# A third late expert: expert 29's results reach token tiles 1 and 0 through TensorE instead of through DRAM

## The chip, the cores and the metric

One core of one Trainium2 chip runs the whole program. The metric is the device time of one execution in microseconds. Engines are named as in the profile: PE is TensorE, DVE is VectorE, ACT is ScalarE, POOL is GpSimd, SP is SyncE, which here only issues DMAs.

## The reference, cut to what matters

Two trunk layers over 256 latent and 256 context tokens, model width 1024. Each layer has a mixer and then a mixture of experts. Layer 0 sends 512 tokens (four tiles of 128) through the experts, layer 1 only the 256 latent ones (tiles 0 and 1). Between them lies layer 1's norm and its input projection; after layer 1 there is only a final norm.

```python
def hierarchical_moe(t, wg, bg, we, be, w1, w3, w2):
    g_logit = (t @ wg + bg); g_sel = argmax(g_logit); g_w = softmax(g_logit)[g_sel]
    e_logit = (t @ we + be).reshape(n, 4, 8)[g_sel]          # 8 experts of the chosen group
    top_p, top_i = lax.top_k(softmax(e_logit), 2)
    top_w = top_p / sum(top_p) * g_w
    for e in range(32):                                       # every token uses two of the 32
        y += combine[:, e] * ((silu(t @ w1[e]) * (t @ w3[e])) @ w2[e])
```

w1, w3 (1024 x 256) and w2 (256 x 1024) are float32, 1 MB each, so one expert is 3 MB of weights.

## The kernel before, in words

The engines run separate programs, written out by hand and tied by semaphores.

**Weights.** SP loads every expert's three matrices as two DMAs of 512 KB each into a ring of 12 slots (`in_ring`, L699). It waits for a free slot (`ring_free`), which PE signals with the first matmul after the last use of a slot. The order is w1, w3 of expert e, then w2 of expert e-1. A few matrices go to spare places loaded ahead.

**One expert.** POOL gathers the rows of up to 64 tokens from DRAM (`gather`, L2523). On PE, `step` (L1154) does for expert e: `T` of the next expert (four transposes, L1067), `Hd` of the previous one (two transposes, L1105), `U` (w1 and w3, 32 matmuls, L1095), `more` (blocks beyond 64 tokens, here three times in all), and `Dn` of the previous expert (w2, 8 matmuls, L1121). ACT and DVE empty PSUM between these. The result goes from PSUM to one of two buffers `YS` by ACT in layer 0 (`copy_y`, L1687) and by DVE in layer 1 (`gated_y`, L2161). POOL scatters it (`scatter`, L2535) to the DRAM tensor `pair_out`, which has for each token one row half per choice.

**The end of the experts.** The results of experts 30 and 31 (`LATE`) do not go to DRAM first. For tiles 1 and 0, DVE builds for each late expert a matrix of one weight per token and slot (`late_slots`, L2163), PE transposes the four of them in one go after `step` of expert 28 (L1176), ACT copies them back (L1691), and in `late_results` (L1180) PE multiplies them with `YS` (L1189) and adds the first choices read back from DRAM (L1194). DVE adds the second choices in `late_pair` (L2202; L2221, L2225, L2226 in layer 0, L2210 and L2217 in layer 1). POOL tells SP (`most_stored`, L2625) when the scatters of experts 0 to 29 have landed, and SP then issues the fetch of the pairs of tiles 1 and 0 (`pairs_back`, L785, four DMAs of 512 KB). In layer 0 POOL scatters experts 30 and 31 after that fetch has landed, for the two context tiles, which SP fetches later (`pairs_stored`).

**The rows of late experts in DRAM.** At the start of the experts of each layer, POOL writes zeros over the rows of the late experts (`late_zeros`, L2539): a memset and one indirect DMA for each late expert (L2544). In layer 0 this stands between the first gathers and the fetch of rows for an extra block of expert 1 (`fetch`, L2559 and L2563), which PE transposes at L1138.

**After layer 0.** PE waits until DVE has updated the first half of tile 0 (L1480), runs fillers (L896), then transposes the normed tiles (L1416).

Of the kernel before, what the change touches and what calls it, by code (L numbers as in the profile page):

```python
# [19 lines left out]
ALU = mybir.AluOpType  # L20
# [263 lines left out]
LATE = (EXPERTS - 2, EXPERTS - 1)  # L284
LATE_TILES = (1, 0)

# [26 lines left out]
def trunk(nc, A):  # L313
# [4 lines left out]
    with ctx:  # L318
# [87 lines left out]
        late_hot = BIASF[:, 512:1024].rearrange("p (t e n) -> p t e n", t=2, e=2)  # L406
        late_T = BIASF[:, 1024:1536].rearrange("p (t e n) -> p t e n", t=2, e=2)
        first_weight = BIASF[:, 1536:1792].rearrange("p (t n) -> p t n", t=2)
# [11 lines left out]
        late_by_choice = small[:, 64:80].rearrange("p (v k t e) -> p v k t e", v=2, k=2, t=2)  # L420
        late_of = small[:, 80:88].rearrange("p (v t e) -> p v t e", v=2, t=2)
# [95 lines left out]
        late_zeroed = sem("late_zeroed")  # L517
        late_hot_ready, late_full, late_ready = sem("late_hot_ready"), sem("late_full"), sem("late_ready")
# [327 lines left out]
        def _(pe):  # L846
# [206 lines left out]
            def experts(l):  # L1053
# [112 lines left out]

                def late_slots():


                    bank = ps[:, 7, :]  # L1170
                    pe.wait_ge(x_y_ready, pe.snap(extras))
                    pe.wait_ge(late_hot_ready, l + 1)
                    for t in (0, 1):
                        for e in (0, 1):
                            at_bank = P * (2 * t + e)
                            mm = pe.transpose(bank[:, at_bank:at_bank + P], late_hot[:, t, e, :], ident)  # L1176
                            freed(mm)
                    mm.then_inc(late_full, 1)

                def late_results():  # L1180

                    banks = {(t, h): open_bank("late", l, t, h) for t, h in LATE_BANKS}
                    pe.wait_ge(late_ready, l + 1)
                    for t in LATE_TILES:
                        for e, expert in enumerate(LATE):
                            pe.wait_ge(y_ready, n0 + expert + 1)
                            for h in (0, 1):
                                p = slice(CAP * h, CAP * (h + 1))
                                mm = pe.matmul(banks[t, h], late_T[p, t, e, :], YS[p, expert % 2, :],  # L1189
                                               start=(e == 0), stop=False)  # L1190
                                freed(mm)
                        for h in (0, 1):
                            pe.wait_ge(y_back[t][h], 16 * (l + 1))
                            close(pe.matmul(banks[t, h], first_weight[:, t, :], back[t][:, D * h:D * h + 512],  # L1194
                                            start=False, stop=True))
# [26 lines left out]
                late_slots()  # L1222
# [3 lines left out]
                Dn(LAST_GROUP, PER_LOOP - 1)  # L1226
                used(LAST_GROUP, PER_LOOP - 1, (2,))
# [317 lines left out]
        def _(act):  # L1545
# [120 lines left out]
            def experts(l):  # L1666
# [13 lines left out]
                def copy_y(i, q):  # L1680
                    n, b = i * PER_LOOP + (n0 + q), q % 2
                    act.wait_ge(y_full, n + 1)

                    act.wait_ge(scattered[b], (i * 2 + (n0 + q) // 2) * 16)
                    if isinstance(i, int) and PER_LOOP * i + q == 1:
                        act.wait_ge(late_zeroed, 32)
                    act.activation(YS[:, b, :], ps[:, 5 + b, :], ACT.Copy).then_inc(y_ready, 1)  # L1687

                def late_slots():
                    act.wait_ge(late_full, l + 1)  # L1690
                    act.activation(late_T.rearrange("p t e n -> p (t e n)"), ps[:, 7, :], ACT.Copy).then_inc(late_ready, 1)  # L1691
# [37 lines left out]
                late_slots()  # L1729
                for q in range(1, PER_LOOP):  # L1730
                    one(LAST_GROUP, q, c[q], ahead=(q + 1 < PER_LOOP))
                if l == 0:
                    copy_y(LAST_GROUP, PER_LOOP - 1)
# [184 lines left out]
        def _(dve):  # L1918
# [126 lines left out]
            def route(l):  # L2045
# [69 lines left out]
                of_late, of_token = choices[:, :, 0:2, LATE[0]:EXPERTS], [P, 2, 2, 2]  # L2115
# [9 lines left out]
            def experts(l):  # L2125
# [29 lines left out]
                def gated_y(i, q):  # L2155
                    n, b = i * PER_LOOP + (n0 + q), q % 2
                    dve.wait_ge(y_full, n + 1)
                    dve.wait_ge(scattered[b], (i * 2 + (n0 + q) // 2) * 16)
                    if isinstance(i, int) and PER_LOOP * i + q == 1:
                        dve.wait_ge(late_zeroed, 64)  # L2160
                    dve.tensor_tensor(YS[:, b, :], ps[:, 5 + b, :], GY, ALU.mult).then_inc(y_ready, 1)  # L2161

                def late_slots():  # L2163


                    dve.wait_ge(routed, l + 1)
                    for t in (0, 1):
                        for e in (0, 1):
                            dve.tensor_scalar(late_hot[:, t, e, :].rearrange("p (h n) -> p h n", h=2),
                                              iota[:, ::-1].unsqueeze(1).broadcast_to([P, 2, CAP]),  # L2170
                                              late_of[:, 1, t, e:e + 1], late_of[:, 0, t, e:e + 1], ALU.is_equal, ALU.mult)
                        ins = dve.tensor_scalar(first_weight[:, t, :], ident, topw[:, t, 0:1], None, ALU.mult)
                    ins.then_inc(late_hot_ready, 1)
# [21 lines left out]
                late_slots()  # L2195
                for q in range(PER_LOOP):
                    one(LAST_GROUP, q, c[q])
                copy_hT(LAST_GROUP, PER_LOOP - 1)
                if l == 1:
                    gated_y(LAST_GROUP, PER_LOOP - 1)  # L2200
# [171 lines left out]
            late_pair(0)  # L2372
            for t in (1, 0):
# [105 lines left out]
        def _(pool):  # L2479
# [25 lines left out]
            def experts(l):  # L2505
# [21 lines left out]
                def scatter(i, q):  # L2527
# [5 lines left out]
                    pool.wait_ge(sidx_ready, n + 1)  # L2533
# [3 lines left out]
                                            oob_is_err=False).then_inc(scattered[b], 16)  # L2537

# [75 lines left out]
                for q in range(PER_LOOP):  # L2614
# [3 lines left out]
                    if q + 1 < PER_LOOP:  # L2618
                        scatter(LAST_GROUP, q - 1)
                pool.wait_ge(late_zeroed, 32 * (l + 1))  # L2620

                for b in (0, 1):
                    pool.wait_ge(scattered[b], 16 * ((n0 + EXPERTS) // 2 - 1))
                stored(pool.snap(extras))
                pool.sem_inc(most_stored, 1)  # L2625
                if l == 0:
# [3 lines left out]
                    for q in (PER_LOOP - 2, PER_LOOP - 1):  # L2630
                        scatter(LAST_GROUP, q)
                    for b in (0, 1):
                        pool.wait_ge(scattered[b], 16 * EXPERTS // 2)
# [36 lines left out]
```

## Time and profile before

| | us |
|---|---|
| median of 3 runs | 1047.36 |
| lowest, highest | 1046.70, 1048.28 |
| the profiled execution, its own time | 1048.56 |
| its span, first to last instruction | 1046.8 |
| PE busy | 970.4 (93%) |
| layer 0: first and last `U` start | 342.06, 579.73 |
| layer 1: first and last `U` start | 800.91, 1022.85 |
| layer 1: fetch of the pairs issued, last late matmul ends | 1029.93, 1040.52 |

Times in the profile count from the start of the span. A row of the timeline gives start, duration, engine, line, operation and how many were merged; in brackets stands how long the engine was idle before it and what released it. A row of the chain gives start, duration, and what the end of the program waited for in that time.

### The profile page before, as it was taken

How to read it: one execution, taken by the hardware profiler on the slowest of the kernel's cores; microseconds unless marked ns; L12 is line 12 of the kernel's file. 1: busy time of each engine (PE TensorE's matmuls, PEld its weight loads, DVE VectorE, ACT ScalarE, POOL GpSimd, SP SyncE). 2: the span in 40 equal slices, each digit the busy share in tenths (PEclk: the TensorE clock that was granted, in tenths of full speed). 3: DMA queues.
4: the chain of work that ended last, by engine and by line, in shares of the span. 5: the costliest groups of instructions: out<-in, count | busy, mean ns of one | idle time of the engine just before them, and what ended most of it. 6: DMA issues, size and time to landing. Idle time of an engine off the chain costs nothing.

```text
span 1046.8 us, 17807 instructions
## 1 busy us (share of the span) xinstructions
PE 970.4 (93%) x6151; PEld 614.8 (59%) x6152; DVE 362.8 (35%) x851; ACT 248.2 (24%) x537; POOL 213.4 (20%) x307
## 2 busy tenths in 40 slices
PE   5999999998998899998989899999998999998896
PEld 3444457545887455555555384877875555555552
DVE  4159493564337111110011370145444222221124
ACT  5110003444334122221221240033132111111112
POOL 1009300110001243332331100000003333333310
PEclk9999999999998899998999999999998999999899
DMA  9984546999715699999999899273646997999996
GB/s 361 307 273 176 198 115 233 315 339 381 293 66 191 228 385 406 406 406 407 407 406 406 320 317 309 81 279 108 223 166 232 389 399 290 407 405 403 404 405 232
DMA packets 129161, 315.95 MB, mean 302 GB/s; under 512 B 28969, under 2 KB 59969, under 8 KB 129076
## 3 DMA queue, kind: packets, MB, share of 16 engines
q1 hardware_dynamic: 113200, 295.98, 75.9%
q0 software_dynamic: 10880, 12.72, 3.6%
q10 hardware_dynamic: 4996, 6.09, 1.6%
q8 instruction: 56, 0.92, 0.3%
q14 instruction: 29, 0.24, 0.1%
HBM read 315.38 MB, written 22.31 MB: 323 GB/s over the span
## 4 chain that ended last, share of the span: by engine, by line
PE 73%; DMA 14%; DVE 5%; issue 3%; SPq 2%; ACT 2%; POOL 0%; POOLq 0%; DVEq 0%
PE ps L1095 17%; PE ps L929 16%; DMA ring<-in_moe_w 9%; PE ps L981 8%; PE ps L1121 8%; PE ps L939 5%; PE ps L883 3%; PE ps L1067 3%; SPq L699 2%; DMA ring<-in_w_mod 1%; PE ps L1248 1%; PE ps L1105 1%; DMA pair_out<-RH,sidx_all 1%; DMA RH<-hrow,sidx_all 1%; PE ps L896 1%
## 5 line engine op out<-in xcount | busy, mean ns | idle before, releaser
L1095 PE MATMUL ps<-ring,RT 128*64 128x256 f32 x2128 | 261.2, 399 | 26.2 <-DMA ring<-in_moe_w 22.6
L1095 PEld LDWEIGHTS ps<-ring,RT 128*64 128x64 f32 x2128 | 164.0, 143 | 98.6 <-issue 29.5
L929 PE MATMUL ps<-RT,ring 128*128 128x512 f32 (+1 forms) x544 | 182.0, 493 | 0.5 <-DVE RT L2244 0.5
L929 PEld LDWEIGHTS ps<-RT,ring 128*128 128x128 f32 x544 | 102.2, 190 | 76.5 <-issue 69.8
L2131 DVE TENSOR_TENSOR RT<-RT,ps 64x256 f32<-64x256 f32 x64 | 27.1, 423 | 275.7 <-ACT RT L1678 275.7
L1121 PE MATMUL ps<-ring,RT 128*64 128x512 f32 x424 | 100.4, 593 | 1.4 <-DVE RT L2137 1.0
L1678 ACT ACTIVATE RT<-ps 64x256 f32<-64x256 f32 x64 | 24.1, 377 | 254.0 <-PE ps L1095 254.0
L2286 DVE SCALAR_TENSOR_TENSOR RAB<-RM,chan,RAB 128x512 f32<-128x512 f32 x120 | 79.7, 746 | 0.0
L2535 POOL DMA_INDIRECT pair_out<-RH,sidx_all x62 | 63.2, 1019 | 54.0 <-POOL sidx_all L2532 54.0
L2511 POOL DMA_INDIRECT RH<-hrow,idx x8 | 8.4, 1046 | 308.5 <-DVE idx L2083 306.7
L2523 POOL DMA_INDIRECT RH<-hrow,sidx_all x56 | 59.0, 1054 | 50.8 <-POOL sidx_all L2520 48.1
L1067 PEld LDWEIGHTS ps<-const,RH 128*128 128x128 f32 x256 | 36.0, 209 | 46.5 <-issue 46.4
L1672 ACT ACTIVATE RT<-ps 128x512 f32<-128x512 f32 x64 | 38.2, 597 | 77.9 <-PE ps L1067 76.3
L939 PE MATMUL ps<-ring,RT 128*128 128x256 f32 x256 | 56.0, 380 | 0.0
L1121 PEld LDWEIGHTS ps<-ring,RT 128*64 128x64 f32 x424 | 32.0, 137 | 38.7 <-issue 31.1
L939 PEld LDWEIGHTS ps<-ring,RT 128*128 128x128 f32 x256 | 48.5, 190 | 7.7 <-issue 1.2
L1067 PE MATMUL ps<-const,RH 128*128 128x128 f32 x256 | 47.8, 311 | 0.0
L2532 POOL COPY sidx_all<-idx 128x1 int32 (+1 forms) x62 | 12.3, 199 | 168.2 <-DVE RH L2161 79.4
L883 PE MATMUL ps<-ring,csilu 128*32 128x256 f32 x768 | 44.1, 381 | 1.9 <-ACT G L1774 1.7
L2137 DVE COPY RT<-ps 128x128 f32<-128x128 f32 x64 | 18.6, 291 | 73.7 <-PE ps L1105 73.6
L981 PE MATMUL ps<-ring,RT 128*128 128x256 f32 x192 | 42.8, 380 | 0.9 <-ACT RT L1549 0.9
L2641 POOL TENSOR_TENSOR RM<-RM,PR 128x512 f32<-128x512 f32 x4 | 28.4, 7111 | 73.8 <-ACT PR L1549 73.8
(271 smaller groups left out, 1005.6 us busy)
## 6 DMA issues: line engine op xcount, KB each, us to landing
ring<-in_moe_w SPq DMA_DIRECT2D x358, 512.0 KB, 14.6
ring<-in_w_mod SPq DMA_DIRECT2D x96, 512.0 KB, 9.2
ring<-in_odd_w_in SPq DMA_DIRECT2D x24, 512.0 KB, 9.4
ring<-in_even_w_in SPq DMA_DIRECT2D x20, 512.0 KB, 9.5
ring<-in_even_w_out SPq DMA_DIRECT2D x8, 512.0 KB, 11.4
RAB<-in_moe_w SPq DMA_DIRECT2D x8, 512.0 KB, 7.9
RAB<-pair_out SPq DMA_DIRECT2D x8, 512.0 KB, 5.8
ring<-in_odd_w_out SPq DMA_DIRECT2D x8, 512.0 KB, 3.9
```

The lines of the kernel that those rows point to most:

```text
L883: mm = pe.matmul(bank[32 * j:32 * j + 32, 0:BLK], csilu[:, c, :], w[:, c % 2, BLK * j:BLK * (j + 1)], start=(c == 0), stop=(c == NCH - 1))
L929: mm = pe.matmul(bank, w[:, c, P * ft:P * (ft + 1)], moving[:, c, :], start=(c == 0), stop=(c == NCH - 1))
L939: mm = pe.matmul(bank[:, BLK * i:BLK * (i + 1)], chunk_of(c, t), w[:, c, :], start=(c == 0), stop=(c == NCH - 1))
L981: mm = pe.matmul(bank[:, BLK * (b % 2):BLK * (b % 2 + 1)], source[:, c % 4, P * t:P * (t + 1)], w[b][:, c, :], start=(c == 0 and b % 2 == ...
L1067: mm = pe.transpose(ps[:, b, P * j:P * (j + 1)], XG[:, q % 4, j:512:4], ident)
L1095: mm = pe.matmul(bank[CAP * k:CAP * (k + 1), 0:BLK], xt(c), w[k][:, BLK * c:BLK * (c + 1)], start=(c == 0), stop=(c == NCH - 1))
L1121: mm = pe.matmul(bank[CAP * k:CAP * (k + 1), :], ht(f), w[:, D * f + 512 * k:D * f + 512 * (k + 1)], start=(f == 0), stop=(f == 1))
L1672: act.activation(XT[:, b, :, :, :].rearrange("p j a s -> p (j a s)"), ps[:, b, :], ACT.Copy).then_inc(xT_ready, 1)
L2286: return dve.scalar_tensor_tensor(out=out, in0=z, scalar=chan[:, ct, k:k + 1], in1=out, op0=ALU.mult, op1=ALU.add)
L2523: pool.indirect_dma_start(out=XG[:, q % 4, :], out_offset=None, in_=hrow[l], in_offset=bass.IndirectOffsetOnAxis(ap=GIDX[q % 4], axis=0), ...
L2535: pool.indirect_dma_start(out=pair_out[l], out_offset=bass.IndirectOffsetOnAxis(ap=SIDX[b], axis=0), in_=YS[:, b, :], in_offset=None, boun ...
L2641: pool.tensor_tensor(z, z, SG[:, ct % 2, :].rearrange("p (s t) -> p s t", s=2), ALU.mult).then_inc(gated_in, 1)
```

## The change

`LATE` becomes experts 29, 30 and 31. Each engine's program for the last group of four experts is rewritten for it, and three buffers take the late results, so that none of them waits for another's use. POOL's wait before `most_stored` now counts the scatters of experts 0 to 28.

```diff
-LATE = (EXPERTS - 2, EXPERTS - 1)
+LATE = (EXPERTS - 3, EXPERTS - 2, EXPERTS - 1)
+SCATTERED = [sum(e % 2 == b for e in range(LATE[0])) for b in (0, 1)]
...
+        late_rows = [XG[:, 0, :], YS[:, 0, :], YS[:, 1, :]]
```

On PE the transposes are three for tile 1 after the step of expert 28, and three for tile 0 inside the step of expert 29, between `U` and `more`, with a wait for ACT's copy behind them. The late products of expert 29 for tile 1 come before the last `Dn`, the first choices last.

```diff
                     U(i, q)
                     if isinstance(i, int) and (i, q) == (LAST_GROUP, 1):
-                        pe.wait_ge(late_ready, l + 1)
+                        late_slots(1, LATE_TILES[1])
+                        pe.wait_ge(late_ready, 2 * l + 2)
...
-                def late_slots():
+                def late_slots(n, t):
                     bank = ps[:, 7, :]
                     pe.wait_ge(x_y_ready, pe.snap(extras))
-                    pe.wait_ge(late_hot_ready, l + 1)
-                    for t in (0, 1):
-                        for e in (0, 1):
-                            at_bank = P * (2 * t + e)
-                            mm = pe.transpose(bank[:, at_bank:at_bank + P], late_hot[:, t, e, :], ident)
-                            freed(mm)
+                    pe.wait_ge(late_hot_ready, 2 * l + n + 1)
+                    if n:
+                        pe.wait_ge(late_ready, 2 * l + n)
+                    for e in range(len(LATE)):
+                        mm = pe.transpose(bank[:, P * e:P * (e + 1)], late_hot[:, t, e, :], ident)
+                        freed(mm)
                     mm.then_inc(late_full, 1)
+                def late_added(banks, t, e):
+                    pe.wait_ge(y_ready, n0 + LATE[e] + 1)
+                    for h in (0, 1):
+                        p = slice(CAP * h, CAP * (h + 1))
+                        mm = pe.matmul(banks[t, h], late_T[p, t, e, :], late_rows[e][p, :], start=(e == 0), stop=False)
+                        freed(mm)
+                def first_choices(banks, t):
+                    for h in (0, 1):
+                        pe.wait_ge(y_back[t][h], 16 * (l + 1))
+                        close(pe.matmul(banks[t, h], first_weight[:, t, :], back[t][:, D * h:D * h + 512],
+                                        start=False, stop=True))
...
+                    late_added(banks, 1, 0)
+                    Dn(LAST_GROUP, PER_LOOP - 1)
+                    used(LAST_GROUP, PER_LOOP - 1, (2,))
+                    late_added(banks, 1, 1)
+                    late_added(banks, 0, 0)
+                    late_added(banks, 0, 1)
+                    late_added(banks, 1, 2)
+                    first_choices(banks, 1)
+                    late_added(banks, 0, 2)
+                    first_choices(banks, 0)
```

`late_zeros` itself is not edited, but it loops over `LATE`, so it issues three indirect DMAs. ACT copies each tile's three transposes (384 columns) in place of all four (512). DVE builds three matrices for each tile, tile 1 first. In layer 0 POOL has three late scatters, with indices read straight from `idx`, and DVE waits for the first of them before it overwrites the buffer of expert 29:

```diff
+                def late_scatter(e):
+                    pool.wait_ge(y_ready, n0 + LATE[e] + 1)
+                    pool.indirect_dma_start(out=pair_out[l],
+                                            out_offset=bass.IndirectOffsetOnAxis(ap=idx[:, 0, 1, LATE[e]:LATE[e] + 1], axis=0),
+                                            in_=late_rows[e], in_offset=None, bounds_check=4 * tokens[l] - 1,
+                                            oob_is_err=False).then_inc(late_scattered[e], 16)
...
             late_pair(0)
+
+            dve.wait_ge(late_scattered[0], 16)
             for t in (1, 0):
                 normed_tile(2, t)
```

## Rows read from the trace of the kernel before

**Rows 1.** The page: what the DMA engines do in 40 slices, and SP's weight loads.
```profile
DMA  9984546999715699999999899273646997999996
...
ring<-in_moe_w SPq DMA_DIRECT2D x358, 512.0 KB, 14.6
```
**Rows 2.** The chain of waits at the start of layer 0's experts.
```profile
345.84 0.99 POOL pair_out L2544
...
348.06 6.24 DMA RH<-hrow,sidx_all
```
**Rows 3.** The timeline of the same place.
```profile
344.52 1.01 POOL L2544 DMA_INDIRECT pair_out<-RH,idx  x1 [0.82 <-POOL RH L2542]
...
354.35 0.74 PE L1138 MATMUL ps<-const,RH 128*128 128x128 f32 x4 [1.37 <-DMA RH<-hrow,sidx_all]
```
**Rows 4.** Stretches of 2 us there: PE clock, DMA share, GB/s stand last.
```profile
358.00:360.00 2.00, 2.00 (x12) 1.20 (x10) 0.00 (x0) 0.00 (x0) 0.00 (x0) 0.50 0.06 18
...
380.00:382.00 2.00, 2.00 (x19) 1.43 (x20) 0.29 (x1) 0.62 (x2) 1.03 (x2) 1.00 1.03 412
```
**Rows 5.** The timeline of PE: `U` of experts 30 and 31 in both layers, and one more.
```profile
571.67 5.32 PE L1095 MATMUL ps<-ring,RT 128*64 128x256 f32 x32 [1.55 <-DMA ring<-in_moe_w]
...
579.73 3.67 PE L1095 MATMUL ps<-ring,RT 128*64 128x256 f32 x32 [0.65 <-DMA ring<-in_moe_w]
...
951.73 3.67 PE L1095 MATMUL ps<-ring,RT 128*64 128x256 f32 x32 [1.67 <-DMA ring<-in_moe_w]
...
1014.92 5.36 PE L1095 MATMUL ps<-ring,RT 128*64 128x256 f32 x32 [1.54 <-DMA ring<-in_moe_w]
...
1022.85 3.67 PE L1095 MATMUL ps<-ring,RT 128*64 128x256 f32 x32 [0.47 <-DMA ring<-in_moe_w]
```
**Rows 6.** The timeline in layer 1: the four late transposes and their copy.
```profile
1004.62 0.66 PE L1176 MATMUL ps<-const,BIAS 128*128 128x128 f32 x4
...
1005.31 0.60 ACT L1691 ACTIVATE BIAS<-ps 128x512 f32<-128x512 f32 x1 [1.92 <-PE ps L1176]
```
**Rows 7.** The chain of waits at the end of layer 0's experts.
```profile
580.44 7.10 DMA pair_out<-RH,sidx_all
...
588.07 4.13 DMA RAB<-pair_out
```
**Rows 8.** The chain of waits at the end of layer 1's experts.
```profile
1023.85 5.56 DMA pair_out<-RH,sidx_all
...
1030.30 5.22 DMA RAB<-pair_out
```
**Rows 9.** The timeline at the end of layer 0's experts, PE and DVE.
```profile
585.88 1.94 PE L1121 MATMUL ps<-ring,RT 128*64 128x512 f32 x8 [0.38 <-DVE RT L2137]
...
592.24 3.60 PE L1194 MATMUL ps<-RAB,BIAS 128*128 128x512 f32 x4 [2.51 <-DMA RAB<-pair_out]
...
594.36 0.75 DVE L2221 SCALAR_TENSOR_TENSOR RAB<-RAB,small,ps 128x512 f32<-128x512 f32 x1 [8.53 <-PE ps L1194]
...
598.85 0.75 DVE L2221 SCALAR_TENSOR_TENSOR RAB<-RAB,small,ps 128x512 f32<-128x512 f32 x1 [0.18 <-PE ps L1194]
...
601.16 4.55 PE L896 MATMUL ps<-const 128*128 128x256 f32 x20 [1.49 <-issue]
```
**Rows 10.** The timeline at the end of layer 1's experts, PE.
```profile
1028.17 0.45 PE L1105 MATMUL ps<-const,RT 64*128 64x64 f32 x2
...
1029.22 1.94 PE L1121 MATMUL ps<-ring,RT 128*64 128x512 f32 x8 [0.60 <-DVE RT L2137]
...
1031.09 1.99 PE L1189 MATMUL ps<-RH,BIAS 64*128 64x512 f32 x8
...
1035.57 1.13 PE L1194 MATMUL ps<-RAB,BIAS 128*128 128x512 f32 x2 [0.32 <-DMA RAB<-pair_out]
1036.62 1.99 PE L1189 MATMUL ps<-RH,BIAS 64*128 64x512 f32 x8
1038.54 1.98 PE L1194 MATMUL ps<-RAB,BIAS 128*128 128x512 f32 x4
```
**Rows 11.** A stretch of 1 us near the end of layer 1's weights, columns as above.
```profile
1027.00:1028.00 1.00, 1.00 (x6) 0.17 (x2) 0.40 (x1) 1.00 (x1) 0.00 (x0) 1.00 0.69 271
```
**Rows 12.** POOL's scatters (L2535) from 560 to 612 us: issue to landing.
```profile
DMA to landing us min/median/max: 2.4/7.1/7.2
```

More of the change, by code:

```diff
@@ L517, in trunk @@
         late_zeroed = sem("late_zeroed")
+        late_scattered = [sem(f"late_scattered{e}") for e in range(len(LATE))]
         late_hot_ready, late_full, late_ready = sem("late_hot_ready"), sem("late_full"), sem("late_ready")
@@ L1180, in late_results @@
                 def late_results():
                     banks = {(t, h): open_bank("late", l, t, h) for t, h in LATE_BANKS}
[L1183 to L1195, printed above, removed]
+                    late_added(banks, 1, 0)
@@ L1221, in experts @@
                 step(LAST_GROUP, 0, c[0])
-                late_slots()
+                late_slots(0, LATE_TILES[0])
                 for q in range(1, PER_LOOP):
@@ L1728, in experts @@
                 one(LAST_GROUP, 0, c[0])
-                late_slots()
+                late_slots(0, LATE_TILES[0])
                 for q in range(1, PER_LOOP):
-                    one(LAST_GROUP, q, c[q], ahead=(q + 1 < PER_LOOP))
+                    if q + 1 < PER_LOOP:
+                        copy_xT(LAST_GROUP, q + 1)
+                    silu(LAST_GROUP, q)
+                    if q == 1:
+                        late_slots(1, LATE_TILES[1])
+                    more(q, c[q])
+                    if l == 0:
+                        if q == 1:
+                            copy_y(LAST_GROUP, 0)
+                        else:
+                            copy_late_y(q - 2)
                 if l == 0:
-                    copy_y(LAST_GROUP, PER_LOOP - 1)
+                    copy_late_y(2)
                 table(ACT.Sqrt)
@@ L2112, in route @@
                 step(dve.tensor_tensor(topw[:, 0:T, 1], rexp[:, 4, 0:T], topw[:, 0:T, 0], ALU.mult))
-                of_late, of_token = choices[:, :, 0:2, LATE[0]:EXPERTS], [P, 2, 2, 2]
+                of_late, of_token = choices[:, :, 0:2, LATE[0]:EXPERTS], [P, 2, 2, len(LATE)]
                 step(dve.tensor_tensor(late_by_choice[:, 0, :, :, :], of_late, topw[:, 0:2, :].rearrange("p t k -> p k t")
@@ L2194, in experts @@
                 c = extra_counts(dve, l, LAST_GROUP)
-                late_slots()
-                for q in range(PER_LOOP):
-                    one(LAST_GROUP, q, c[q])
+                for t in LATE_TILES:
+                    late_slots(t)
+                one(LAST_GROUP, 0, c[0])
+                for q in range(1, PER_LOOP):
+                    copy_hT(LAST_GROUP, q - 1)
+                    hidden(LAST_GROUP, q)
+                    more(q, c[q])
+                    if l == 1:
+                        if q == 1:
+                            gated_y(LAST_GROUP, 0)
+                        else:
+                            gated_late_y(q - 2)
                 copy_hT(LAST_GROUP, PER_LOOP - 1)
                 if l == 1:
-                    gated_y(LAST_GROUP, PER_LOOP - 1)
+                    gated_late_y(2)
             def late_pair(l):
@@ L2629, in experts @@
                             pool.wait_ge(y_back[t][h], 16)
[L2630 to L2633, printed above, removed]
+                    for e in range(len(LATE)):
+                        late_scatter(e)
+                    for e in range(len(LATE)):
+                        pool.wait_ge(late_scattered[e], 16)
                     pool.sem_inc(pairs_stored, 1)
```

59 lines of the change are left out of this document (33 added, 26 removed).

## The prediction

> **What bounds the kernel now.** I read the page first, then the chain of waits, then the timeline and short stretches at both ends of both layers' experts. The page shows the DMA engines full through most of both expert phases [rows 1]: there the weights set the pace, and PE waits about half a microsecond to two for them before each `U` [rows 5]. The change touches none of those bytes. So it can only move three stretches: the start of layer 0's experts, where PE waits for POOL's gather; the end of layer 0's experts up to layer 1's projection; and the end of layer 1. At both ends the chain reads: scatter of expert 29 (7.10 and 5.56 us), the fetch of the pairs (4.13 us for its first quarter in layer 0, 5.22 for its second in layer 1), first choices on PE, DVE [rows 7, 8]. The change aims at this chain. The reader should ask what is late next once the fetch comes early.
>
> **Removed: the wait for the scatter of expert 29.** Expert 28's scatter goes one step of 8 us (1014.92 to 1022.85, [rows 5]) before that of expert 29: near 1016 in layer 1 and 572.5 in layer 0. With the same landing times [rows 7, 8] the fetch can be issued near 1021.5 and 579.5, where today the scatter of 29 lands at 1029.41 and 587.54. Its 2 MB then stand behind weights that SP has already queued; those take 14.6 us from issue to landing [rows 1], which is a queue worked off in order. In layer 1 weights still keep 0.69 of the DMA engines busy at 1027 [rows 11], so the first quarter lands near 1030 to 1031 and the second about 1.3 later, against 1035.5 now. In layer 0 it is near 588 to 590 against 592.2 and later. After that the end is not set by the fetch but by PE, so the rest is a count of PE work behind the last `U`.
>
> **Prices on PE.** With two late products per pair, four pairs (call one `la`) stand where the trace has two. In [rows 10] one half first choice takes 1.05 from 1035.57 to 1036.62, two `la` take 1.92 to 1038.54, and a whole first choice takes 1.98 with its drain. A change of kind costs some 0.19 and a whole first choice 1.72 without drain (four matmuls of 0.43), so one `la` is 0.86. A `Dn` takes 1.87 from start to the next start (1029.22 to 1031.09).
>
> **End of layer 1.** One `la` (0.86 and 0.15 for the change) goes in before the last `Dn`, which today waits 0.60 for DVE's copy [rows 10]: `Hd` begins at 1028.17 and takes 0.38, so `Dn` starts at 1029.56, 0.34 later. Behind it: `Dn` 1.87, four `la` 3.44 and 0.19, first choices of tile 1 1.72 and 0.19, one `la` 0.86 and 0.19, first choices of tile 0 1.98, together 10.4. The end is 1039.97 against 1040.52: **-0.55**. All behind it (DVE's last update, the final norm, the store) hangs on this end. So 1.3 us of waiting are removed, but one more `la` per tile and a delay of `Dn` are paid on the same engine. Bounds: +0.4, if each `la` costs a whole 0.96 and `Dn` waits 0.6 more; -1.4, if the added products fully hide, as PE's two waits (1.03 and 0.32) go.
>
> **End of layer 0.** The same count from 585.88 [rows 9]: there `Hd` and one `la` push `Dn` by 0.56 to 586.44. `Dn` 1.87, four `la` 3.63, then half a first choice with drain 1.12: DVE can begin at 593.1 instead of 594.36. DVE is the bound from there: half a tile takes 2.12 (three operations), 4.24 for two, so the third half starts at 597.4 instead of 598.85 (4.49 after the first, as DVE waited). The fillers at L896 wait for that third update, and the norm of tile 0 for the fourth, so layer 1's projection moves by 1.46. But this execution is dear here: the four L1194 took 3.60 against 1.98 for the same four at the full clock, PE having idled 2.51 before [rows 9, 10]. In an execution without that, DVE starts at 593.5 and the gain is about 0.46. I take **-1.0**; bounds -1.5 and 0.
>
> **Start of layer 0: a third zero DMA.** The pitch of two such DMAs is 1.32 (344.52 to 345.84) [rows 2, 3]. The third goes in on POOL ahead of the fetch for expert 1's extra block, at 348.06. That fetch lands 6.24 later, and PE is already idle 1.37 for it [rows 2, 3], so there is no cover: PE starts the block 1.32 later. Is the loss made up by the DMA bound? No: at 358 to 360 the DMA engines stand at 0.06, the ring being full until PE frees a slot; at 380 they are full [rows 4] and stay so to the end of the layer [rows 1]. A later restart shifts all. So **+1.32**; bounds 0 (if the gather lands no later) and +3.0 (the `U` behind it also loses up to 1.7 more at the low clock of 1.2 GHz, the difference of 5.36 and 3.67 [rows 5]). In layer 1 the same DMA delays gathers that are used 20 us later: 0.
>
> **Late transposes.** Tile 0's three now stand between `U` and `Dn` of the step of expert 29, with a wait for ACT's copy: at most 0.66 and 0.60 [rows 6], some 1.2. `Dn` of 28, `T` and `Hd` are queued behind it. PE waits 1.55 and 1.54 for weights before the next `U` [rows 5], and the weights are not delayed, since the loads still outstanding use slots freed earlier. So 0; without that cover it would be 1.2 in each layer. DVE's two more matrices, the wider router products and ACT's split copy stand beside waits of PE for weights: 0, at worst 0.3 each.
>
> **What this does to the clock.** `U` of expert 30 ran 5.3 us at the low clock after 1.55 and 1.54 of idle, that of 31 3.67 after 0.65 and 0.47; elsewhere 1.67 of idle left it at 3.67 [rows 5], so it is chance. With the late transposes filling the idle before `U` of 30, that one stays fast and ends 1.7 earlier, and the idle before `U` of 31 grows to some 2.2. If that one then runs at the low clock, it adds 1.7 behind which nothing waits any more; today such a loss would lie under the wait for the fetch. I give it one in three in each layer. It is not in the sum, but it is in the range.
>
> **Other new waits.** DVE's wait for the scatter of expert 29 in layer 0 comes behind the fourth update, near 602. The scatter is issued once the fetch has landed, some 593, and takes 2.4 to 7.2 us [rows 12]: landed by 601. No cost, 2 at worst. The context tiles are fetched no later than now.
> The Trainium skill, "DMA: Bandwidth & Descriptors", section "Queues, rings and completion order", says that each DMA engine takes turns between the queues of the issuing engines, packet by packet, while one queue is consumed in ring order. By its first half the scatter, on POOL's queue, shares the engines with projection weights that SP now issues earlier, and is near the slow end: the sum stays, the margin shrinks to 1 us. By a single queue for all it would be behind 2 MB, and the sum would be 2 higher. The trace has 2.4 us for a scatter on idle engines and 7.1 under weights, which agrees with the taking of turns [rows 12].
>
> **Sum.** +1.32 -1.0 -0.55 = -0.23 us. Against the profiled execution's own 1048.56 that is 1048.3. That execution lies 1.2 above the median of 1047.36, so I forecast 1047.1 us for the median, no change that can be measured (about 0.2%, 2.1 us, is the least that can).
>
> **Rivals and their chances.**
> - *Likeliest, 0.48:* as summed, 1047.1; alone its range is 1046.0 to 1048.2.
> - *The end moves onto `U` of expert 31, 0.20:* it runs at the low clock, often enough to show in the median, in one layer (1048.8) or in both (1050.5). For it: 1.5 of idle sufficed three times before. Against: 1.67 once did not.
> - *Slower, the fetch takes DMA time from the last weights, 0.07:* 2 MB move at some 400 GB/s in 5.2 us. If they are not held behind the queue, the last w2 comes up to 5 us later than about 1027.8. `Dn` has 1.7 of room, so it decides from there: some 3.3 in each layer, 1053.4. Against it: 14.6 us of queue, and a steady pace.
> - *DVE waits for the first late scatter, 0.07:* 2 us, 1049.1.
> - *The change does not do what it says, 0.08:* the fetch, queued behind weights, lands hardly earlier, and only the added work stays: 1047.4 + 1.3 + up to 0.9 = 1048.7 to 1049.6.
> - *Faster, 0.10:* the third zero DMA is hidden and layer 0 gains its whole 1.5: -2.1, 1045.3. For it: the profiled execution itself has that 1.5. Against: 1.37 of idle without cover.
>
> Below 1045.3 lie half of the last, and 0.06 from the tail of the first: faster 0.12. Above 1049.4 lie the third rival, half of the second, some of the fourth and fifth: slower 0.20. The rest, 0.68, is no change. The range that holds 8 in 10 is 1045.2 to 1049.9.
>
> **What would show it.** After: L2544 three times, and L1138 with some 2.7 of idle instead of 1.37; L785 issued near 1021.5 and 579.5, plus the shifts; no idle before L1194; L1105, L1189 and L1121 in this order before the last `Dn`; `U` of 30 at 3.67, and `U` of 31 with 2 us of idle before it. I am wrong if the fetch is not issued before 1025, if the last w2 lands late, if L1946 in layer 0 waits for POOL, or if the time between the last `Dn` and the last L1194 is not 10.4.

## The result and the profile after

Over 14 runs of each, the changed kernel takes 1050.33 us (median; 1046.63 to 1054.25), the kernel before 1047.98. The ratio is 1.0032, 95% interval 1.0019 to 1.0046: slower by 3.3 us (2.0 to 4.8). The difference of the two medians, 2.35, lies inside that interval. The forecast had no change and 1045.2 to 1049.9; the result is 0.4 above that, and the kernel before itself stands 0.62 above the 1047.36 on which the forecast was built. The profiled execution took 1051.01 with a span of 1049.3, against 1048.56 and 1046.8.

First the timeline at the start of layer 0's experts, as in [rows 2, 3].

```profile
346.39 1.01 POOL L2601 DMA_INDIRECT pair_out<-RH,idx  x1 [0.82 <-POOL RH L2599]
347.70 0.99 POOL L2601 DMA_INDIRECT pair_out<-RH,idx  x1 [0.30 <-issue]
349.00 0.98 POOL L2601 DMA_INDIRECT pair_out<-RH,idx  x1 [0.30 <-issue]
...
351.23 1.07 POOL L2620 DMA_INDIRECT RH<-hrow,sidx_all  x1 [0.90 <-POOL sidx_all L2616]
...
357.85 0.75 PE L1143 MATMUL ps<-const,RH 128*128 128x128 f32 x4 [2.33 <-DMA RH<-hrow,sidx_all]
359.29 5.36 PE L1100 MATMUL ps<-ring,RT 128*64 128x256 f32 x32 [0.69 <-ACT RT L1724]
```

There are three zero DMAs and 2.33 of idle in place of 1.37. This execution's first `U` began 1.95 later than before's (344.01 against 342.06), in a stretch that the change does not touch; the extra block begins 3.50 later. So 1.55 was lost here, and the last `U` of layer 0 is 3.63 later.

The timeline of the last two `U` of either layer, as in [rows 5], with SP's issue of the fetch:

```profile
575.50 3.67 PE L1100 MATMUL ps<-ring,RT 128*64 128x256 f32 x32
583.24 1.75 SPq L790 DMA_DIRECT2D RAB<-pair_out  x4
583.36 3.67 PE L1100 MATMUL ps<-ring,RT 128*64 128x256 f32 x32 [2.09 <-DMA ring<-in_moe_w]
...
1016.45 3.67 PE L1100 MATMUL ps<-ring,RT 128*64 128x256 f32 x32
1024.19 5.36 PE L1100 MATMUL ps<-ring,RT 128*64 128x256 f32 x32 [1.96 <-DMA ring<-in_moe_w]
1024.37 1.75 SPq L790 DMA_DIRECT2D RAB<-pair_out  x4
```

`U` of expert 30 no longer waits, and that of 31 waits 2 us; in layer 1 it ran at the low clock. The fetch comes 5.6 us earlier than before in layer 1 (1024.37 against 1029.93).

The chain of waits at the end of layer 1, as in [rows 8]:

```profile
1007.68 16.38 DMA ring<-in_moe_w
...
1024.19 5.36 PE ps L1100 x32
...
1032.56 1.87 PE ps L1126 x8
1034.42 3.63 PE ps L1192 x16
1038.06 1.91 PE ps L1199 x4
1039.97 1.06 PE ps L1192 x4
1041.03 1.93 PE ps L1199 x4
```

Scatter and fetch have left the chain. From the last `Dn` (1032.49 in the timeline) to the last drain (1042.94) it is 10.45, forecast 10.4. The end of the experts is 2.42 later than before's 1040.52, 1.34 of it there already at the last `U`.

The timeline at the end of layer 0's experts, as in [rows 9]:

```profile
595.48 1.99 PE L1199 MATMUL ps<-RAB,mod_rows 128*128 128x512 f32 x4
596.64 0.75 DVE L2268 SCALAR_TENSOR_TENSOR RAB<-RAB,small,ps 128x512 f32<-128x512 f32 x1 [7.18 <-PE ps L1199]
...
598.45 1.98 PE L1199 MATMUL ps<-RAB,mod_rows 128*128 128x512 f32 x4
603.16 4.55 PE L901 MATMUL ps<-const 128*128 128x256 f32 x20 [2.73 <-issue]
607.55 1.91 PE L1433 MATMUL ps<-const,RH 128*128 128x128 f32 x16
```

The first choices wait for nothing; the last are done at 600.43, and PE idles 2.73 before the fillers, where it was 1.49. Here the stretch from the last `U` to the projection is 24.19, 1.63 less than the 25.82 of before. So this one profile says +1.55, -1.63, +1.08 at the end of layer 1 and 0.4 within its experts, which together is +1.4 (the rest of the 2.5 between the spans lies in stretches that the change does not touch); the ratio says 3.3. One profile of each kernel does not show where the loss is.

### The profile page after: what moved, and what is told of

It is laid out like the page before. It is cut to its first block, busy times and chain, and to the rows that moved or that the text cites. A ratio compares the mean times of both kernels' runs of the same rounds, so it can differ in the third digit from the quotient of the medians.

```text
span 1049.3 us, 17861 instructions
## 1 busy us (share of the span) xinstructions
PE 971.7 (93%) x6171; PEld 615.0 (59%) x6172; DVE 363.3 (35%) x855; ACT 249.4 (24%) x539; POOL 214.0 (20%) x304
## 4 chain that ended last, share of the span: by engine, by line
PE 70%; DMA 14%; DVE 5%; SPq 4%; issue 4%; ACT 2%; POOL 0%; ACTq 0%; POOLq 0%; DVEq 0%
PE ps L934 16%; PE ps L1100 15%; DMA ring<-in_moe_w 13%; PE ps L986 8%; PE ps L1126 7%; PE ps L944 5%; SPq L704 4%; PE ps L888 3%; PE ps L1072 2%; PE ps L1265 1%; DMA RH<-hrow,sidx_all 1%; PE ps L1110 1%; PE ps L1192 1%; PE ps L922 1%; PE ps L901 1%
## 5 line engine op out<-in xcount | busy, mean ns | idle before, releaser
L1695 ACT ACTIVATE RT<-ps 64x256 f32<-64x256 f32 x64 | 24.2, 378 | 253.2 <-PE ps L1100 253.2
L2584 POOL DMA_INDIRECT pair_out<-RH,sidx_all x58 | 59.3, 1022 | 50.6 <-POOL sidx_all L2581 50.6
L944 PEld LDWEIGHTS ps<-ring,RT 128*128 128x128 f32 x256 | 48.5, 190 | 7.7 <-issue 1.2
L986 PEld LDWEIGHTS ps<-ring,RT 128*128 128x128 f32 x192 | 36.2, 190 | 6.5 <-ACT RT L1566 1.2
```

Of the source, the lines that this page charges most:

```text
L944: mm = pe.matmul(bank[:, BLK * i:BLK * (i + 1)], chunk_of(c, t), w[:, c, :], start=(c == 0), stop=(c == NCH - 1))
L986: mm = pe.matmul(bank[:, BLK * (b % 2):BLK * (b % 2 + 1)], source[:, c % 4, P * t:P * (t + 1)], w[b][:, c, :], start=(c == 0 and b % 2 == ...
L2584: pool.indirect_dma_start(out=pair_out[l], out_offset=bass.IndirectOffsetOnAxis(ap=SIDX[b], axis=0), in_=YS[:, b, :], in_offset=None, boun ...
```

## The stretches in all profiles

Each experiment left a profile. These are differences of start times from the timelines, us. "Block": first `U` of layer 0 to `Hd` of the extra block. "To last U": first to last `U` of the layer. "To projection": last `U` of layer 0 to the first transposes of layer 1's projection. "Tail": last `U` of layer 1 to the end of the last late matmul. The ratio is to the kernel before on the same chip, from five rounds each (all runs for the first two rows).

| kernel | block | L0 to last U | to projection | L1 to last U | tail | ratio (95%) |
|---|---|---|---|---|---|---|
| before | 20.11 | 237.67 | 25.82 | 221.94 | 17.67 | 1 |
| after | 21.66 | 239.35 | 24.19 | 222.34 | 18.75 | 1.0032 (1.0019-1.0046) |
| b_again | 19.98 | 237.50 | 24.77 | 221.86 | 17.77 | 1.0000 (0.9980-1.0020) |
| a_again | 23.48 | 241.23 | 25.59 | 222.55 | 17.07 | 1.0039 (1.0022-1.0055) |
| a_third | 23.49 | 241.40 | 25.58 | 222.71 | 17.07 | 1.0025 (1.0010-1.0039) |
| b_three_zeros | 21.82 | 239.73 | 24.04 | 222.41 | 17.66 | 1.0033 (1.0017-1.0049) |
| a_fill | 23.12 | 240.90 | 24.19 | 223.77 | 17.06 | 1.0031 (1.0016-1.0046) |
| a_extra_fill | 20.21 | 237.83 | 25.88 | 226.41 | 17.07 | 1.0035 (1.0019-1.0052) |
| a_extra_third | 19.23 | 236.82 | 24.20 | 225.22 | 17.06 | 1.0022 (1.0008-1.0037) |
| a_zeros_later | 17.61 | 235.32 | 27.44 | 222.14 | 17.07 | 0.9987 (0.9971-1.0004) |
| az_again | 17.56 | 235.28 | 25.67 | 221.90 | 17.07 | 0.9977 (0.9963-0.9991) |
| az_third | 16.63 | 234.35 | 24.19 | 222.05 | 17.08 | 0.9978 (0.9958-0.9998) |
| az_fetch_late | 17.40 | 235.15 | 25.57 | 221.99 | 17.07 | 0.9980 (0.9965-0.9994) |
| az_fillers | 17.00 | 234.89 | 24.62 | 222.14 | 17.07 | 0.9967 (0.9951-0.9983) |
| az_best | 16.99 | 234.95 | 22.95 | 222.88 | 17.08 | 0.9972 (0.9956-0.9988) |
| b_zeros_later | 16.63 | 234.13 | 24.38 | 222.12 | 17.66 | 0.9968 (0.9956-0.9981) |
| bz_again | 16.53 | 234.46 | 25.06 | 222.11 | 17.61 | 0.9968 (0.9950-0.9986) |
| bz_third | 17.35 | 235.45 | 26.21 | 222.28 | 17.66 | 0.9970 (0.9954-0.9986) |

## The experiments

Theory A: the third zero DMA costs what is lost. Theory B: the end moved onto the `U` of expert 31 at the low clock. Theory C: the fetch takes DMA time from the last weights.

### The changed kernel again (a_again, a_third)

> The changed kernel as it is, once more, for a second profile of it. All theories: 1.001 to 1.005 of the kernel before. Theory A (the third zero DMA): the extra block of expert 1 in layer 0 waits over 2 us for its rows again, where the kernel before waited 1.37, and the shift of 1.3 to 1.6 us stays to the end of that layer. Theory B (the end moved onto the U of expert 31): it starts after about 2 us of idle in both layers and takes 5.36 us at the low clock in some layer, 3.67 at the full one; where it takes 5.36, the end comes 1.7 later. Theory C (the fetch takes DMA time from the last weights): the idle before the U of expert 31 is over 3 us, or the last Dn waits for its w2.

1.0039, and 1.0025 in a later session (a_third, quoted further down). The timeline of a_again:

```profile
357.24 1.03 PE L1143 MATMUL ps<-const,RH 128*128 128x128 f32 x4 [3.44 <-DMA RH<-hrow,sidx_all]
...
603.84 5.95 PE L901 MATMUL ps<-const 128*128 128x256 f32 x20 [2.73 <-issue]
609.63 1.91 PE L1433 MATMUL ps<-const,RH 128*128 128x128 f32 x16
```

The extra block waits 3.44, its transposes take 1.03 for 0.75, and it ends 1.8 later after the first `U` than in the first profile of the same kernel. The same 20 fillers take 5.95 and end 1.4 later, with the norms as early as before. The short stretches show why (PE's clock, DMA share and GB/s stand last); first the changed kernel's first profile:

```profile
603.20:605.20 2.00, 2.00 (x10) 1.77 (x11) 1.93 (x4) 0.91 (x3) 0.00 (x0) 1.00 0.35 98
```

and a_again:

```profile
603.20:605.20 2.00, 1.36 (x3) 1.17 (x4) 1.93 (x4) 1.02 (x3) 0.00 (x0) 0.52 0.11 27
```

After the same 2.73 of idle the granted clock is 1.00 in one execution and 0.52, the lower level of 1.2 GHz, in the other. Theory C is out: the idle before `U` of 31 is 1.94 and 2.10, under 3.

### A third zero DMA alone (b_three_zeros)

```diff
-                    for e in LATE:
+                    for e in (EXPERTS - 3,) + LATE:
```

with the waits on the zeros counted up (48 and 96 for 32 and 64). Nothing else of the change.

> The kernel before with one thing of the change: a third indirect DMA of zeros (over the rows of expert 29, which its own scatter writes again later) at the start of both layers' experts. Theory A: 1.3 to 1.8 us slower than the kernel before (ratio 1.0012 to 1.0017), with the extra block in layer 0 waiting 2.3 to 2.7 us for its rows, where it was 1.37. Theories B and C: no change (within 0.3 us).

1.0033: as slow as the whole change, some 3.5 us, and more than Theory A's 1.3 to 1.8 (the interval, 1.0017 to 1.0049, just reaches them).

```profile
351.06 1.07 POOL L2563 DMA_INDIRECT RH<-hrow,sidx_all  x1 [0.90 <-issue]
...
357.17 0.75 PE L1138 MATMUL ps<-const,RH 128*128 128x128 f32 x4 [2.46 <-DMA RH<-hrow,sidx_all]
358.61 5.36 PE L1095 MATMUL ps<-ring,RT 128*64 128x256 f32 x32 [0.69 <-ACT RT L1700]
...
1023.56 5.36 PE L1095 MATMUL ps<-ring,RT 128*64 128x256 f32 x32 [2.14 <-DMA ring<-in_moe_w]
```

The last row shows another thing. Here the last `U` ran at the low clock after 2.14 of idle, and the tail is 17.66 as with a fast one (17.67): in the kernel before, the wait for the fetch covers that loss, as the forecast said.

### The zeros behind the gathers, in the changed kernel (a_zeros_later, az_again, az_third)

```diff
-                late_zeros()
                 for q in range(PER_LOOP):
...
+                    if q == 0:
+                        late_zeros()
```

> The changed kernel with all three zero DMAs moved on POOL behind the fetch of expert 1's extra block and the gather behind it. Theory A: 1.3 to 1.8 us comes back, and as the two older zero DMAs leave the path too, up to 2.6 more, but no more than the 2.3 us of idle that the extra block had: 2 to 2.5 us faster than the changed kernel (ratio to the kernel before about 1.001). Theory B: the start of layer 0 matters little, what is left of the loss (up to 1.7 a layer) stays. If POOL's order does not matter because the DMA engines catch up: as the changed kernel.

> The changed kernel with the zero DMAs behind the gathers once more, as the base for the two kernels beside it and for what the change is worth without them. 0.997 to 1.000 of the kernel before, as the last time (0.9987).

> The same kernel without that edit, as its base (0.998 of the kernel before). By theory D its fillers take about 6 us and the projection starts 25.6 us after the last U of layer 0.

The ratios are 0.9987, 0.9977 and 0.9978, on average 0.9981, against 1.0032 of the changed kernel: 5.3 us back, twice what was expected. The bound of "no more than the idle it had" left out PE's clock. The block shrinks from 21.7 to 23.5 down to 16.6 to 17.6, since its `U` also takes 3.67 instead of 5.36 to 6.46.

### The zeros behind the gathers, in the kernel before (b_zeros_later, bz_again)

> The kernel before with its two zero DMAs moved behind the fetch of expert 1's extra block. Theory A, as it now stands (the start of layer 0 alone explains the loss, by the idle and by the low clock behind it): from the first U to the end of the extra block's U about 16.6 us where the kernel before has 19.1, so 2.5 us faster than the kernel before or a little more (1045 to 1046.5, ratio 0.997). The rest of the change is then worth the difference to the changed kernel with the same move: by the forecast 1.55 us in favour of the change; if the late work on PE and the low clock at the U of expert 31 eat it, none or less than none, and this kernel is the fastest so far.

```profile
345.00 1.03 POOL L2563 DMA_INDIRECT RH<-hrow,sidx_all  x1 [0.87 <-POOL sidx_all L2559]
...
352.57 0.75 PE L1138 MATMUL ps<-const,RH 128*128 128x128 f32 x4
354.00 3.67 PE L1095 MATMUL ps<-ring,RT 128*64 128x256 f32 x32 [0.69 <-ACT RT L1700]
```

The fetch goes out 2.9 us after the first `U` instead of 6.0 [rows 2], the rows are there in time, and the `U` runs at full clock. 0.9968, 0.9968 and 0.9970 in three sessions: 3.3 us faster than the kernel before, from an edit that moves one call. The table has 2.9 of it in layer 0 (237.6 to 234.7 on average). This kernel beats both. The changed kernel with the same move is 1.3 us behind it by these averages; each interval is 1.5 us to either side, so that difference is likely but not settled by itself. (a_zeros_later ran on another chip than the other five; without it the difference is 0.9.)

### Fillers before the last U (a_fill)

```diff
+                    if isinstance(i, int) and (i, q) == (LAST_GROUP, PER_LOOP - 1):
+                        pe.wait_ge(x_y_ready, pe.snap(extras))
+                        for _ in range(4):
+                            pe.matmul(ps[:, 7, 0:BLK], ident, const[:, 0:BLK], start=True, stop=True)
```

> The changed kernel with eight filler instructions (four f32 products, 1.8 us) on PE between Hd of expert 30 and the U of expert 31, in the idle that the late transposes left there. Theory B: this U stays at 3.67 us in both layers and up to 1.7 us a layer come back, 0.5 to 1.7 us in the median. Theory A and C: no change, 0.3 us at most. If the fillers outlast the wait for weights: slower by the overlap, up to 0.3 a layer.

```profile
1024.06 1.99 PE L1167 MATMUL ps<-const 128*128 128x256 f32 x8
1026.16 3.67 PE L1100 MATMUL ps<-ring,RT 128*64 128x256 f32 x32
```

1.0031 beside 1.0039 on the same chip. `U` stays fast, but it mostly did so without them: of ten profiles with three late experts and nothing in this place, one has a slow last `U` in layer 1 (after) and two in layer 0 (a_zeros_later, az_fillers). The eight do not quite fit the idle: no wait is left behind them, and layer 1 to the last `U` is 223.8 here against 222.3 to 222.7 in the changed kernel, and 222.9 in az_best against 221.9 to 222.1 in its bases. They are not all of that difference: from the `U` of expert 30 to that of 31 it is 7.80 here and 7.65 to 7.74 in the changed kernel (7.62 in az_best, 6.94 to 7.58 in its bases). The `U` of 30 already began 0.9 later than in any profile of the changed kernel, and the fillers leave no wait in which that could be made up.

### Fillers before the extra block (a_extra_fill, a_extra_third)

```diff
+                            if l == 0 and isinstance(i, int) and i == 0:
+                                for _ in range(5):
+                                    pe.matmul(bank[:, 0:BLK], ident, const[:, 0:BLK], start=True, stop=True)
                             pe.wait_ge(x_gathered, x * 16)
```

> The changed kernel, zeros where they were, with ten filler instructions (2.5 us) on PE in the idle before the extra block of layer 0. The rows come no earlier. If the cost of the third zero DMA is the 1.3 us of waiting alone: as the changed kernel. If PE's low clock after the long idle is the larger part: the U of the extra block takes 3.67 us instead of 5.36 to 6.30, its transposes 0.75 instead of 1.03, and 1.7 to 2.9 us come back.

The first run came out at 1.0035, level with the changed kernel, although its profile shows the gain in layer 0. A second one stands beside the changed kernel:

> The changed kernel as it is, as the base of the next one. 1.003 to 1.004 of the kernel before; the Hd of the extra block starts 21.7 to 23.5 us after the first U.

> The changed kernel with ten fillers in the idle before the extra block of layer 0, once more. If half the cost of the third zero DMA is the low clock behind the idle: Hd of the extra block 20.2 us after the first U as in its first profile, the U of the extra block 3.67 us, and 1.5 to 2.5 us back in the median. If it is the later rows alone: level with the changed kernel, as the medians of the first try had it.

```profile
356.81 2.43 PE L1143 MATMUL ps<-const 128*128 128x256 f32 x10
359.07 0.63 PE L1146 MATMUL ps<-const,RH 128*128 128x128 f32 x4
360.39 3.67 PE L1100 MATMUL ps<-ring,RT 128*64 128x256 f32 x32 [0.69 <-ACT RT L1727]
...
855.30 1.05 POOL L2623 DMA_INDIRECT RH<-hrow,sidx_all  x1 [0.88 <-POOL sidx_all L2619]
...
863.12 0.75 PE L1146 MATMUL ps<-const,RH 128*128 128x128 f32 x4 [1.79 <-DMA RH<-hrow,sidx_all]
864.56 5.07 PE L1100 MATMUL ps<-ring,RT 128*64 128x256 f32 x32 [0.69 <-ACT RT L1727]
```

In layer 0 both profiles confirm the clock: with PE kept at work, it is 6.1 and 6.0 from the block's transposes to its `Hd`, where the changed kernel has 7.8 to 9.1, and the block takes 20.2 and 19.2 in place of 21.7 to 23.5, though the zeros stand where they were, and layer 0 to the last `U` falls from 240.7 (mean of three) to 237.3. But in layer 1 both lose 2.7 to 3.9 at its own extra block, which waits 1.8 and 2.0 for its rows (0.3 to 0.5 in all others), with a low clock behind. The edit adds no work in layer 1, and why its gather lands later stays open. With that the times come out level (1.0022 and 1.0025, and 1.0035 in the first run).

### The fetch held back (az_fetch_late)

```diff
+                pool.wait_ge(y_ready, n0 + EXPERTS - 1)
                 pool.sem_inc(most_stored, 1)
```

> The changed kernel with the zeros behind the gathers, and the fetch of the pairs held back until the result of expert 30 is there, about when the kernel before issued it (7 us after the start of the last U). If the early fetch is what the change brings: PE waits again before the first choices, up to 1 us a layer, 1 to 2 us slower. If PE's own late work covers the fetch either way: within 0.5 us; by the landing time of before (5.2 us for the second quarter) against the late products in front of it on PE, 0.4 us of waiting in layer 1.

The timeline in layer 1, az_again first:

```profile
1020.33 1.75 SPq L790 DMA_DIRECT2D RAB<-pair_out  x4
```

```profile
1026.51 1.75 SPq L790 DMA_DIRECT2D RAB<-pair_out  x4
...
1031.97 1.98 PE L1199 MATMUL ps<-RAB,mod_rows 128*128 128x512 f32 x4
```

Issued 6.2 us later (6.7 after the last `U` began, 0.4 earlier than in the kernel before), the fetch is still there when PE wants it, with no idle: 0.9980 and 0.9977, tail 17.07 in both. With the four late products per half in front of the first choices, PE covers the fetch by itself. In layer 0 it went out 6.9 later (583.56 against 576.63), also with no wait. Once the late work stands in front of the first choices, the earlier fetch that the change is for brings nothing more.

### The fillers after layer 0 earlier (az_fillers)

```diff
-            pe.wait_ge(x_updated, xu_moe[0] - 5)
-            warm(("xT", LATENT, 0), 10)
+            pe.wait_ge(x_updated, xu_moe[0] - 6)
+            warm(("xT", LATENT, 0), 12)
```

> The changed kernel with the zeros behind the gathers, and after layer 0 the fillers of PE start after DVE's second update instead of its third (0.5 us after PE's last first choices, where it now idles 2.73), four more of them (24 instructions). Theory D: in four of six profiles of the changed kernel the 20 fillers took 5.95 to 6.03 us instead of 4.55, having started at the low clock after that idle, and layer 1's projection came 1.4 later. Then these 24 take 5.5 us, the projection starts 24.2 us after the last U of layer 0 in place of 25.6, and 1 us comes back (1.45 in two executions of three). If the projection waits for the norms anyway: no change.

> The kernel before with its zero DMAs behind the gathers once more: 0.997 of the kernel before. Theory D: its fillers take 4.55 us (idle before them 1.5), the projection starts 24.0 to 24.4 after the last U, so this kernel stays 0.5 to 1 us ahead of the changed kernel with the same move; with the earlier fillers the changed kernel draws level or passes by 0.3 us (the 0.6 us at the end of layer 1, less the executions with a slow last U).

> The kernel before as it is, for a second profile. Ratio 1.000. The extra block's idle in layer 0 is 1.4 to 2.1 us (POOL issued the fetch 6.0 us after the first U in the first profile, and 7.2 to 7.9 us in those with three zero DMAs, 1.3 of it for the third), its U 5.36 to 5.9; the projection starts 24.0 to 25.8 after the last U of layer 0, and the end of layer 1's experts 17.67 after its last U at either clock.

az_fillers has 0.9967 where its base az_third has 0.9978. In the profile of az_fillers the last `U` was slow (1.7), and the projection still comes at 24.62, where a_zeros_later, slow in the same place, had 27.44. But az_third's one profile happened to have fast fillers, and the two medians are 1044.08 and 1044.03: the gain in time is not shown. The slow fillers that Theory D starts from are there: with the three late experts, 20 fillers after 2.73 of idle took 4.55 in four profiles and 5.93 to 6.24 in six; with two, after 1.48, they took 4.55 in six of six. The second profile of before (b_again), with a longer wait at the extra block than the first, and PE's wait for the fetch's quarter as one of 1.19:

```profile
354.33 0.75 PE L1138 MATMUL ps<-const,RH 128*128 128x128 f32 x4 [2.19 <-DMA RH<-hrow,sidx_all]
...
593.27 1.13 PE L1194 MATMUL ps<-RAB,BIAS 128*128 128x512 f32 x2 [1.19 <-DMA RAB<-pair_out]
...
599.71 4.55 PE L896 MATMUL ps<-const 128*128 128x256 f32 x20 [1.48 <-issue]
```

### All three repairs (az_best, bz_third)

a_zeros_later, a_fill and az_fillers in one kernel, beside the kernel before with its zeros moved.

> The changed kernel with all three repairs: zeros behind the gathers, the earlier fillers after layer 0, and eight fillers before the last U. All last Us at 3.67 us, projection 24.2 us after it, 17.07 from it to the end. Against the kernel before with moved zeros (projection after 24.0 to 25.8, tail 17.6 to 17.8) that is 0.6 us at each end: 0.9960 to 0.9965 of the kernel before, 0.3 to 1.2 us under bz_third. If the change is worth nothing even so: level with bz_third.

> The kernel before with its zero DMAs behind the gathers, as the base: 0.9968 of the kernel before.

```profile
595.95 5.42 PE L901 MATMUL ps<-const 128*128 128x256 f32 x24 [0.61 <-issue]
601.21 2.14 PE L1437 MATMUL ps<-const,RH 128*128 128x128 f32 x16
```

The projection comes at 22.95, the earliest of all, but layer 1 to the last `U` is longer (222.88), in part by the fillers in front of it. The ratios are 0.9972 and 0.9970: level. The plain medians, 1045.53 and 1047.01, would have az_best 1.5 ahead; the ratios have it 0.2 behind, each to 1.7 us, so a gain of the forecast size (0.3 to 1.2) is neither shown nor ruled out. Even with its side effects repaired the third late expert is worth nothing that these runs can tell; the profit that is shown is in the moved zeros.

## Why the prediction was wrong, step by step

**Start of layer 0: +1.32, measured +3.1 in the traces (237.6 to 240.7 on average), which is the miss.** Place, sign and pitch were right: 1.30 from one zero DMA to the next. The step that failed is the equation of cost and later issue, "PE starts the block 1.32 later". The chance of more stood in it as a bound only (+3.0), priced as a `U` that falls from 3.67 to 5.36. In the kernel before that `U` is at the low clock already (its timeline; the stretch at 358 to 360 in [rows 4] has 0.50):

```profile
355.78 5.36 PE L1095 MATMUL ps<-ring,RT 128*64 128x256 f32 x32 [0.69 <-ACT RT L1700]
```

So that 1.7 could not be lost a second time. What a longer wait did was to leave the block at the low clock for longer: with three zero DMAs the block's transposes and its `U` took 0.75 and 5.36 in two profiles (2.33 and 2.46 of idle), and up to 1.13 and 6.46 in three (2.84 to 3.44 of idle), against 0.75 and 5.02 to 5.36 in the kernel before. From the transposes to `Hd` that is 7.8 to 9.1 instead of 7.5 to 7.8, some 0.9 on average. The other part is the wait: the transposes begin 14.2 after the first `U` instead of 12.4, 1.8 for 1.3, as POOL's memset began 0.6 later after the first `U` in four of these five profiles and in neither of the two of before. That looks like a draw and not like the change: a_extra_fill and a_extra_third, also with three zero DMAs, do not have it, and with the zeros moved the fetch goes out 2.8 to 3.1 or 3.5 after the first `U`, with two late experts and with three. That a third zero DMA costs the whole loss is shown by the time of b_three_zeros (its one profile has +2.1 in layer 0 and +0.5 in layer 1); the split into wait and clock is read from the profiles.

**End of layer 0: -1.0, measured about +0.2** (25.05 on average for six profiles with two late experts, 24.0 to 26.2; 25.25 for the ten with three and 20 fillers, 24.2 to 27.4). The gain of 1.0 is not there; with such a spread the sign of what is there is not settled. DVE's start and its third update moved as worked out. What failed is the clause that the fillers "wait for that third update", taken as a fixed 4.55 behind it. PE now ends its own work 1.2 earlier against DVE's third update and idles 2.73 in place of 1.49, and the fillers that are to raise the clock began low themselves in six of ten profiles, at 1.4 each; the projection stands behind them, not behind the norms. On the other side, before's slow L1194 [rows 9], which I priced at half of the 1.0, was no rule (3.60 once, 2.35 once, not in the other four).

**End of layer 1: -0.55, measured -0.43.** Tail 17.67 to 17.07, which is -0.60, in nine of ten, and 18.75 in one. The count of PE work and its order were right.

**The last U at the low clock: one in three in each layer, measured three in twenty.** The mechanism is real (18.75, and 17.66 with the cover), but it was the wrong place to put the chance of a slower result: the same thing happened at two idle times to which the forecast gave none.

**Layer 1's zeros: 0, measured about 0.5** (222.5 in three profiles of the changed kernel, 222.4 in b_three_zeros, 221.9 in before, 221.9 to 222.3 with zeros moved). One place is in the timelines: from the first `U` of layer 1 to the second it is 5.56 to 6.13 in five of the seven profiles with three zero DMAs in front, where ACT begins its work behind the first `U` later, and 5.13 to 5.15 in all others. But the changed kernel's first profile has 5.14 there and is 0.4 longer all the same, so the cause stays open.

**Others.** Late transposes at no cost: right, `U` of 30 had no idle and that of 31 came on time. Their wait for ACT is 1.16. The fetch: forecast near 1021.5 and 579.5 plus the shifts, it went out at 1024.37 and 583.24, which with the shifts of the last `U` (1.34 and 3.63) is 1.5 and 0.1 later. The forecast left out that the late transposes hold up `Dn` of 28, and so its scatter: in layer 0 this `Dn` starts 5.31 instead of 3.48 after the `U` of 29. The forecast's times for that scatter were too late by nearly as much, which made up for it: in before it goes out at 570.81 and 1014.15, not near 572.5 and 1016. As az_fetch_late shows, that did not matter. The late scatters went out at 597.57 rather than near 593 (596.6 with the shift), as the fetch's last quarter landed later than I had it; they took 2.7 to 7.5 to land, and still DVE did not wait for the first. The fetch took nothing from the last weights.

The measured segments add up: +3.1, +0.2, +0.5 and -0.4 are +3.4, beside 3.3 by the first ratio. That they agree so well is partly luck, with three profiles of the changed kernel and two of before behind the largest. The 0.20 that the forecast gave to a slower result stood for other reasons, above all the last `U`; none of them makes up the loss. The sum was made from one profile of before, which had the shortest wait at the extra block (1.37, 2.19 in the second).

## What to carry to other kernels

A wait that PE already has on the critical path costs more than its length when it grows: price what follows it at both clock levels, and take the chances from several profiles of the same kernel, since one shows only one draw. Look at the idle times that the change makes longer, also where PE only gets ready early for another engine. And where a step adds work in front of a late DMA, try first to move it behind: here one moved call was worth 3.3 us, the change itself nothing that could be measured.

## What the runs showed of the hardware

- Idle time and clock are not tied firmly. After the same 2.73 of idle PE worked on at the full clock in four executions and low in six. The last `U` was slow in 3 of 20 cases with three late experts (idle before it 1.17 to 2.58), and in 6 of 8 with two where its idle was 2.14 to 2.71.
- The gather of layer 1's extra block, issued 53.7 to 54.3 after the layer's first `U` each time, was in use 6.4 to 6.5 us after its issue in the changed kernel (859.35 to 865.77 in a_third) and 7.8 to 8.1 after it in the kernel with ten more fillers in layer 0 (855.30 to 863.12), both times that this one was profiled.
